# Down projection: the places of the four weight-panel slots in SBUF

## The reference, cut to what matters

```
u = _causal_dwconv(_rmsnorm(h, norm2_g[l]) @ w_up[l], mlp_conv_w[l])
u_gate, u_up = jnp.split(u, 2, axis=-1)
h = h + (jax.nn.silu(u_gate) * u_up) @ w_down[l]
...
return _rmsnorm(h, final_norm_g)[:, N_META:]
```

## The kernel before

| operand | place(s) modulo 256 |
|---|---|
| DN, moving, `hi` and `lo`, panels 0 to 3 | 128 |
| DN, moving, `hi` and `lo`, panels 4 to 87 | 112 |
| DN, stationary, `act_h` / `act_l` | 224 or 224 / 96 or 96 |
| BR to UP, stationary, tiles of `hi` and `lo` | 128 |
| BR to UP, moving, rows j = 0 to 3, window of 258 or 260 columns | 80, 144, 208, 16 |
| BR to UP, moving, rows j = 0 to 3, window of 272 columns | 32, 96, 160, 224 |

## Time and profile before

### The profile page before, as it was taken

The page is one execution under the profiler, slowest core; times in us unless marked ns, Lnnn a source line. Parts: engine busy times, 40 slices in busy tenths (PEclk is TensorE's granted clock), DMA queues, the critical chain, the costliest instruction groups (busy, mean ns, idle before and its releaser), DMA issues.

```text
span 1726.3 us, 34115 instructions
## 1 busy us (share of the span) xinstructions
PE 1716.1 (99%) x13429; PEld 1665.4 (96%) x13429; DVE 1117.4 (65%) x1605; ACT 764.1 (44%) x921; POOL 263.2 (15%) x492
## 2 busy tenths in 40 slices
PE   9999999999999999999999999999999999999998
PEld 8999999999999999999999999999999999888886
DVE  6857767667565554555556687777777777554454
ACT  6635454354354444444444443344444444433443
POOL 4153333630530000000000044321000000000000
PEclk9999999999999999999999999999999999999999
DMA  8566557566565555565655566666555565655554
GB/s 235 171 181 188 168 153 200 174 167 180 159 184 187 179 173 189 175 203 183 194 174 184 187 198 207 205 201 189 185 184 186 187 191 182 224 194 191 189 192 136
DMA packets 310297, 320.63 MB, mean 186 GB/s; under 512 B 17354, under 2 KB 285134, under 8 KB 310094
## 3 DMA queue, kind: packets, MB, share of 16 engines
q1 hardware_dynamic: 296861, 311.01, 57.8%
q0 software_dynamic: 12928, 7.80, 2.1%
q10 hardware_dynamic: 432, 0.79, 0.1%
HBM read 311.10 MB, written 2.11 MB: 181 GB/s over the span
## 4 chain that ended last, share of the span: by engine, by line
PE 99%; DVE 0%; DMA 0%; ACT 0%; SPq 0%; issue 0%; ACTq 0%; DVEq 0%
PE ps L1436 81%; PE ps L1714 5%; PE ps L1713 5%; PE ps L1712 5%; PE ps L1543 1%; DMA xb<-in_x_dram 0%; PE ps L1557 0%; PE ps L1582 0%; PE ps L1572 0%; PE ps L1573 0%; PE ps L1601 0%; PE ps L1602 0%; DVE xl L941 0%; DVE lo L896 0%; PE ps L1474 0%; PE ps L1529 0%
## 5 line engine op out<-in xcount | busy, mean ns | idle before, releaser
L896 DVE TENSOR_TENSOR lo<-raw,hi 128x1024 fp32r<-128x1024 f32 x584 | 710.0, 1230 | 477.7 <-ACT hi L627 475.9
L627 ACT CAST hi<-raw 128x1024 fp32r<-128x1024 f32 x584 | 605.1, 1049 | 654.3 <-PE ps L1436 520.6
L1436 PE MATMUL ps<-xh,hi 128*128 128x260 f32 (+2 forms) x3312 | 530.3, 282 | 0.2 <-DVE xl L941 0.2
L1436 PE MATMUL ps<-xl,hi 128*128 128x260 f32 (+2 forms) x3312 | 527.6, 281 | 0.0
L1436 PE MATMUL ps<-xh,lo 128*128 128x260 f32 (+2 forms) x3312 | 527.3, 281 | 0.0
L1436 PEld LDWEIGHTS ps<-xh,hi 128*128 128x128 f32 x3312 | 450.5, 188 | 1.4 <-issue 0.4
L1436 PEld LDWEIGHTS ps<-xl,hi 128*128 128x128 f32 x3312 | 450.5, 188 | 0.0
L1436 PEld LDWEIGHTS ps<-xh,lo 128*128 128x128 f32 x3312 | 450.2, 188 | 0.0
L610 POOL DMA_DIRECT2D hT<-h2b x128 | 69.4, 551 | 597.6 <-DVE h2b L1286 592.0
L1714 PE MATMUL ps<-lo,act_h 128*128 128x512 f32 x350 | 137.5, 393 | 0.0
L1713 PE MATMUL ps<-hi,act_l 128*128 128x512 f32 x350 | 136.9, 391 | 0.0
(11 more groups left out here) (300 smaller groups left out, 1249.2 us busy)
## 6 DMA issues: line engine op xcount, KB each, us to landing
raw<-in_w_in_dram SPq DMA_DIRECT2D x224, 512.0 KB, 3.5
raw<-in_w_up_dram SPq DMA_DIRECT2D x176, 512.0 KB, 4.7
raw<-in_w_down_dram SPq DMA_DIRECT2D x88, 512.0 KB, 4.5
raw<-in_w_o_dram SPq DMA_DIRECT2D x32, 512.0 KB, 3.3
raw<-in_w_in_dram SPq DMA_DIRECT2D x32, 256.0 KB, 4.0
raw<-in_w_a_o_dram SPq DMA_DIRECT2D x16, 512.0 KB, 4.2
raw<-in_w_b_o_dram SPq DMA_DIRECT2D x16, 512.0 KB, 3.2
raw<-in_w_c_o_dram SPq DMA_DIRECT2D x16, 512.0 KB, 3.2
```

The lines of the kernel that those rows point to most:

```text
L627: nc.scalar.copy(part(ph, i, q, hi_all), raw[:, s, :]).then_inc(hi_ready, 1)
L896: nc.vector.tensor_tensor(part(ph, i, q, lo_all), raw[:, s, :], part(ph, i, q, hi_all).bitcast(F32), ALU.subtract).then_inc(lo_ready, 1)
L1436: ins = nc.tensor.matmul(acc, tiles(weights, s, j, m), moving(j)[side][:, a:], start=first and (kind, at) == (0, 0), stop=last and (kind, ...
```

## The change

From panel 4 of the down projection on, slot s of `hi` moves a further (3 - s) times 16 numbers ahead, and slot s of `lo` (3 - s) times 32 numbers. Slot 3 stays. In bytes ahead of where they are now, slots 0 to 3: `hi` 192, 128, 64, 0; `lo` 384, 256, 128, 0.

```
+DSTEP = 16
...
-            at = DPAD + ph.slot(q) * KJ * COLS - (DAT if ph is DN and i * DN.n + q >= SLOTS else 0)
+            s = ph.slot(q)
+            step = 2 * DSTEP if buf is lo_all else DSTEP
+            at = DPAD + s * KJ * COLS - (DAT + (SLOTS - 1 - s) * step if ph is DN and i * DN.n + q >= SLOTS else 0)
```

## The result

The change made the kernel slightly slower: 1730.89 us (median of 20 runs, 1730.36 to 1732.87) against 1728.56 us (20 runs, 1728.25 to 1729.31), a ratio of 1.0014 with a 95% interval of 1.0007 to 1.0020, which leaves out 1. The forecast was 1724.8 us. The time stayed inside the range that was given, on the other side of "before".

The account below looks back on a forecast made before the run. TensorE, busy 1716.1 of 1726.3 us, was taken as the bound. 5.7 ns saved on each of 756 products gave 4.3 us, with nothing for casts, loads or slot 3: 1729.08 - 4.3 = 1724.8 us, range 1721.5 to 1732.5.

Parts of the forecast that it names:

- rival 1: Down projection: place counts only modulo 64 or less, pace stays 228.9 ns, 1729.1 us; no or little change had 0.27.
- The bounds of the sum: Slots 0 to 2 from panel 4 on, 756 products: at best 4.8 us saved, at worst 3.2 us lost.
- the excess of the three earlier stages: Time over streaming in up projection, branch and gate stages, mean 9.9 ns; applied to 756 down-projection products, 4.3 us saved.
- Slot 3: I take nothing: Slot 3 of the down projection, 246 products at the same addresses: neighbours' timing could move it a little, priced at nothing.
- One fixed distance can be a bad one for every product, four can't all be: Down projection: reason for expecting places taken in turn to be faster, 5.7 ns saved on each of 756 products.
- rival 2: Down projection: place 112 is a favourable distance, slots 0 to 2 lose 4.3 us, 1733.4 us; slower had 0.18.
- The turned order: Gate stage: after its row order turns, five groups take 2.39 us, then 2.36; taken as evidence that 64 bytes count, 1.5 ns.

Follow-up runs that it names:

- shift_all: Kernel before with `hi` and `lo` of all slots from panel 4 on, and the activations, 64 bytes ahead: 1728.6 us.
- equal_places: Kernel before with slots 0 to 3 from panel 4 on at 336, 256, 80 and 0 bytes ahead, `hi` and `lo` alike: 1732.6 us.
- The last two experiments: Kernel before, `hi` reaching 80 bytes ahead by 16 every four panels (1727.69 us), or after panels 4 to 7 at 64 (1726.69 us).
- hi_steps: Kernel before with only `hi` stepped, slots 0 to 3 at 192, 128, 64, 0 bytes ahead, `lo` in place: 1731.5 us.
- The scans: Kernel before, 16 bytes further every four panels: both operands, `hi`, `lo`, or both with `lo` 128 further; 1732.2, 1731.1, 1730.7 and 1731.1 us.
- u_256: Kernel before with `hi` and `lo` of all four slots from panel 4 on 256 bytes ahead: 1728.7 us.
- hi_128: Kernel before with `hi` 128 bytes ahead in all slots from panel 4 on, `lo` in place: 1729.7 us.
- scan_both: Kernel before with `hi` and `lo` together moving 16 bytes further ahead with every four panels from panel 4 on: 1732.2 us.
- hi_80: Kernel before with `hi` 80 bytes ahead in all four slots from panel 4 on, `lo` in place: 1730.94 us against 1729.04.
- short_path_to_80: Kernel before with `hi` 64 bytes ahead in panels 4 to 7, then 80 for the rest, `lo` in place: 1726.69 us against 1728.69.

## Why the prediction was wrong

**Right.** The bound, and that only TensorE's pace could move. That the place counts beyond 64 bytes: it does, modulo 256, and rival 1 is out. That the stationary operand's place counts beside the moving one's, as panels 0 to 3 of shift_all show. Nothing lost in casts, splits or loads: the cast still takes 1.05 us, VectorE's busy time is 1116.8 us (1117.4 before), the DMA share is 0.59 as before. The bounds of the sum (4.8 us saved, 3.2 us lost on the shifted slots) held the 2.0 us that these slots lost.

**The step that failed** is the choice between those bounds. The prediction took the excess of the three earlier stages, 9.9 ns, as what places taken in turn would bring, and so 5.7 ns off for 756 products. Measured over 213.3 ns of streaming, slots 0, 1 and 2 have an excess of 19.0, 17.1 and 18.6 ns, up from 15.6. Alone their places have 17.8, 16.7 and 18.9. The rows of the earlier stages step their places inside a fixed order of four, with the stationary operand always on one place and half the columns. None of that is so here. Taking places in turn brought nothing in this stage: the changed kernel (231.3 ns) is slower than the mean of its four places run alone (230.6), and equal_places (231.2) lost by the sequence that its place 80 fell into. The low excess of the earlier stages is theirs; why they have it stays open. (In the trace's nanoseconds the gate stage has 118.3 and an excess of 10.0, where the rounded rows gave 9.7; the forecast hardly depends on it.)

**"Slot 3: I take nothing"** failed too. Its pace went from 228.9 to 230.3 ns with no address changed: 1.4 ns times 246 products, 0.35 us of the loss. The prediction named the neighbours' timing and priced it at nothing. The last two experiments show that the products ahead can set the pace of those behind. They need not: in hi_steps slot 3 kept 228.8 ns.

**"One fixed distance can be a bad one for every product, four can't all be"** had the odds the wrong way round. The scans have 60 pairs with a mean of 231.6 ns; before's 228.9 is among the best five. By these readings a move from such a place without a reason for the new one loses 2.7 ns on average, an estimate, since a reading can depend on its history; the change lost 2.4. The reason to expect this stood in the earlier trace rows: the one other place that the trace showed was 4.2 ns worse. The forecast used that as a sign that places matter; only rival 2 took it as a sign that before's place was a good one.

**Rival 2** had the direction and half the mechanism, that the slots leave a favourable distance. Its price was too high, 1733.4 us: the slots fell back by 1.5 to 3.5 ns and not by 5.7.

**The earlier trace rows was read for half of what it says.** The turned order was taken as evidence that 64 bytes count. It was also the first sight of a transition: after a change of order the products need a while to find their repeating sequence. The last two experiments add that which one they find can depend on where they come from.

**The mechanism.** Shown: a shift by 256 bytes changes nothing (u_256, hi_128), smaller ones of the moving and of the stationary operand change the pace, and the same places can hold more than one repeating sequence. Not shown: that the distance alone decides. Only argued: that the moving read and the weight load get in each other's way in the memory. So it is known that the new places were slower ones, and not why a given pair is slow.

## What to carry to other kernels

When TensorE is the bound and its products are spaced wider than their columns need, read the start-to-start sequence, not only its mean. A pattern that repeats to 1 or 2 ns for hundreds of microseconds, whatever the other engines do, points at TensorE's own operand reads. Then the addresses modulo 256 bytes of the moving and the stationary operand are worth a scan, for a small prize: the best kernel here gained 2.0 us of 1728.7.

Scan many places in one kernel, a group of panels each, and confirm the chosen one in a kernel of its own, since a pace measured behind other places need not come back without them. Before's layout was among the best of those read, so moving away from it needed a measured value for the new place, and not a value from a stage with other operands.

## What the runs showed of the hardware

- Back-to-back products of 512 float32 columns at a granted clock of 1.00 took 226.7 to 234.4 ns in the first four scans with nothing changed but SBUF addresses, in steps of 16 bytes; 256 bytes further the readings repeat (u_256, hi_128, scan_both).
- With the moving operands in place, moving the stationary ones by 64 bytes took panels 0 to 3 from 233.1 to 231.1 ns (shift_all).
- The repeating sequences have sums that are multiples of 6.67 ns, the time of 16 columns at 2.4 GHz: three products take 680 ns (226.7 each), 700 (233.3), nine take 2060 (228.9), six take 1380 (230.0) or 1387 (231.1). No theory here explains it.
- The same addresses and instructions ran at 231.1 or 226.7 ns a product for 954 products, and all that differed were the addresses of the 48 products ahead of them (hi_80 and short_path_to_80).
- Casts, splits, loads and evacuations beside the products left no mark in these sequences: on places that stay fixed they repeat to 1 ns (before: 2 ns) from panel 9 on, over some 200 us, whatever ScalarE and VectorE do.
